# Two output projections computed third by third, with the feed-forward norm cut into parts between the products

## What is computed

```python
for li in range(2):
    h = rmsnorm(y, attn_norm[li])
    m = mixer_ab(h, ...) if li == 0 else mixer_c(h, ...)   # both end with  out @ w_out  (1024 x 1024)
    y = y + m                                              # <- the output projection
    y = y + swiglu(rmsnorm(y, ffn_norm[li]), ffn_w_in[li], ffn_w_out[li])   # <- the norm after it
y = rmsnorm(y, final_norm)

def rmsnorm(x, g):
    return x * rsqrt(mean(x * x, axis=-1) + 1e-6) * g
```

## Time and profile before

| | |
|---|---|
| three timed runs | 3367.0 us median, 3360.1 to 3375.76 us |
| profiled execution | span 3367.8 us; the page gives no time for it apart from the span |
| TensorE | 3161.1 us busy, 94% of the span |
| VectorE, ScalarE, GpSimd busy | 1456.8, 727.1, 96.9 us |
| chain that ended last | TensorE has 89% of it, VectorE 5% |

### The profile page before, as it was taken

The page is one execution under the profiler, slowest core; times in us unless marked ns, Lnnn a source line. Parts: engine busy times, 40 slices in busy tenths (PEclk is TensorE's granted clock), DMA queues, the critical chain, the costliest instruction groups (busy, mean ns, idle before and its releaser), DMA issues.

```text
span 3367.8 us, 45153 instructions
## 1 busy us (share of the span) xinstructions
PE 3161.1 (94%) x17988; PEld 3004.2 (89%) x17988; DVE 1456.8 (43%) x2451; ACT 727.1 (22%) x1160; POOL 96.9 (3%) x88
## 2 busy tenths in 40 slices
PE   6997989997999999999899999996979999999997
PEld 5996456797999999999799999996979999999996
DVE  6887333325333333333545455454352333333335
ACT  3121445513111111111311111220131111111111
POOL 3000000001000000000100000000010000000001
PEclk9998958998999999999899999996989999999998
DMA  3112410110111111110201111100201111111111
GB/s 120 45 44 70 153 41 1 69 44 32 45 41 41 44 44 44 44 39 32 94 33 39 39 40 39 40 33 21 100 26 56 38 39 45 44 39 44 38 44 57
DMA packets 47748, 163.11 MB, mean 48 GB/s; under 512 B 8416, under 2 KB 15888, under 8 KB 44768
## 3 DMA queue, kind: packets, MB, share of 16 engines
q1 hardware_dynamic: 42992, 148.45, 13.1%
q10 hardware_dynamic: 3456, 8.91, 0.7%
q0 software_dynamic: 1136, 3.27, 0.5%
HBM read 143.28 MB, written 18.92 MB: 48 GB/s over the span
## 4 chain that ended last, share of the span: by engine, by line
PE 89%; DVE 5%; issue 2%; ACT 2%; POOL 1%; DMA 1%; DVEq 0%; POOLq 0%; ACTq 0%; SPq 0%
PE PS L513 19%; PE PS L514 19%; PE PS L515 19%; PE PS L755 5%; PE PS L757 5%; PE PS L756 5%; PE PS L1406 4%; PE PS L1136 2%; PE PS L1167 2%; DVE HF L624 1%; PE PS L1149 1%; PE PS L1160 1%; PE PS L1118 1%; POOL SQ L425 1%; DVE HBL L634 1%
## 5 line engine op out<-in xcount | busy, mean ns | idle before, releaser
L513 PE MATMUL PS<-HAH,WH 128*128 128x384 f32 x1872 | 649.6, 347 | 27.0 <-issue 9.7
L514 PE MATMUL PS<-HAL,WH 128*128 128x384 f32 x1872 | 634.4, 339 | 0.0
L515 PE MATMUL PS<-HAH,WL 128*128 128x384 f32 x1872 | 633.8, 339 | 0.0
L513 PE MATMUL PS<-HBH,WH 128*128 128x384 f32 x1872 | 626.3, 335 | 0.0
L514 PE MATMUL PS<-HBL,WH 128*128 128x384 f32 x1872 | 626.2, 335 | 0.0
L515 PE MATMUL PS<-HBH,WL 128*128 128x384 f32 x1872 | 626.1, 334 | 0.0
L501 DVE TENSOR_TENSOR WL<-WR,WH 128x1024 fp32r<-128x1024 f32 x200 | 243.0, 1223 | 568.5 <-ACT WH L496 567.0
L513 PEld LDWEIGHTS PS<-HAH,WH 128*128 128x128 f32 x1872 | 358.4, 191 | 29.1 <-issue 19.9
L514 PEld LDWEIGHTS PS<-HAL,WH 128*128 128x128 f32 x1872 | 358.6, 192 | 9.7 <-issue 8.7
L755 PE MATMUL PS<-UH,WH 128*128 128x384 f32 x1056 | 360.3, 341 | 5.2 <-issue 5.0
L756 PE MATMUL PS<-UL,WH 128*128 128x384 f32 x1056 | 359.0, 340 | 0.0
(11 more groups left out here) (200 smaller groups left out, 2776.0 us busy)
## 6 DMA issues: line engine op xcount, KB each, us to landing
WR<-w_fi_in SPq DMA_DIRECT2D x88, 512.0 KB, 3.6
WR<-w_fo_in SPq DMA_DIRECT2D x44, 512.0 KB, 3.5
WR<-w_c_in SPq DMA_DIRECT2D x32, 512.0 KB, 4.2
WR<-w_ab_in SPq DMA_DIRECT2D x20, 512.0 KB, 3.6
CACHES<-k_cache_in SPq DMA_DIRECT2D x8, 1024.0 KB, 6.8
CACHES<-v_cache_in SPq DMA_DIRECT2D x8, 1024.0 KB, 5.0
X<-x_t_in SPq DMA_DIRECT2D x3, 1536.0 KB, 10.7
x_spill<-X SPq DMA_DIRECT2D x1, 4608.0 KB, 12.3
```

The costliest lines, as they stand in the source:

```text
L513: nc.tensor.matmul(out, wh, hh(k, third(n)), start=(k == 0), stop=False)
L514: nc.tensor.matmul(out, wh, hl(k, third(n)), start=False, stop=False)
L515: mm = nc.tensor.matmul(out, wl, hh(k, third(n)), start=False, stop=(k == KT - 1))
```

## The change

The projection now goes third by third. For third 0 all 8 output blocks run, then for third 1, then for third 2: 24 products in straight code, with no loop. The weights of every block are therefore loaded, and cut into high and low parts, three times (24 loads of 512 KB instead of 8 in each layer), and each load serves one product. Two PSUM banks take turns (3 and 4) instead of six.

While third n is projected, the norm of third n-1 runs in parts, one part behind each product: m=0 folds the last squares and sums, m=1 takes the root, makes the diagonal and spreads it, m=2 and m=3 scale, m=4 and m=5 split high and low; m=4 to m=7 square and fold what is finished of the running third. VectorE does all folds; GpSimd's `fold_pair` is now called twice instead of four times. The norm of third 2 falls into the first block of the feed-forward part, whose products stand in a new order: a0, sums, b0, spread, a1, b1, a2, b2.

```diff
         def proj_sp(sp, T, w):
-            with sp.Fori(0, KT // 2 - 1) as i:
...
+            for p in range(2, N3 * KT):
+                weights(sp, T, p % 2, w[p % KT, :, :])
...
-            for norm in range(4):
-                fold_pair(2 * N3 + N3 + norm * 2 * N3)
+            for norm in range(2):
+                fold_pair(2 * N3 + N3 + 3 * N3 + norm * (2 + 3) * N3)
...
         def proj_pe(pe, T, ready):
...
+            for p in range(N3 * KT):
+                n, m = divmod(p, KT)
+                have(pe, T, p % 2)
+                if m == 0:
+                    ready(n)
+                need(pe, s_x, T("x") - 1)
+                T.add("x")
+                product(PS[:, 3 + p % 2, 0:TH], p % 2, n).then_inc(s_xo, 1)
+                if n and m == 0:
+                    rms_sums(pe, T, n - 1)
+                if n and m == 1:
+                    rms_cast(pe, T, n - 1)
+
+        SQ_PARTS = (slice(0, 4), slice(4, 6), slice(6, 8))
+
+        def part_squares(act, T, n, part):
+
+            act.wait_ge(s_x, T("x0") + n * KT + SQ_PARTS[part].stop)
+            if part == 0:
+                need(act, s_ms, T("ms"))
+                T.add("ms")
+            ks = SQ_PARTS[part]
+            act.activation(SQ[:, ks, :], X[:, ks, third(n)], ACT.Square).then_inc(s_sq, 1)
+
+        def part_root(act, T, n):
+            act.wait_ge(s_ms, T("ms"))
...
+        def part_hi(act, T, n, half):
+            hf = HF1 if n % 2 else HF0
+            out = (HAH, HBH)[half]
+            T.add("hf")
+            act.wait_ge(s_hf, T("hf"))
+            act.activation(out[:, :, third(n)], hf[:, half * AB:(half + 1) * AB, :], ACT.Copy).then_inc(s_hhi, 1)
+
+        def proj_act(act, T, stored=None):
+
+            T.add("x0", T("x") - T("x0"))
+            for p in range(N3 * KT):
+                n, m = divmod(p, KT)
+                cut_hi(act, T, 1 - p % 2, None if p == 0 else (s_xo, T("x")))
+                T.add("x", 1)
+                if p == 4 and stored:
+                    stored()
+                if n and m == 0:
+                    part_squares(act, T, n - 1, 2)
+                if n and m == 1:
+                    part_root(act, T, n - 1)
+                if n and m == 3:
+                    part_hi(act, T, n - 1, 0)
+                if n and m == 4:
+                    part_hi(act, T, n - 1, 1)
+                if m == 4:
+                    part_squares(act, T, n, 0)
+                if m == 6:
+                    part_squares(act, T, n, 1)
+
+        def part_fold(dve, T, part):
...
+        def proj_dve(dve, T, reloaded, gain):
+            for p in range(N3 * KT):
+                n, m = divmod(p, KT)
+                cut_lo(dve, T, 1 - p % 2)
+                if n and m == 0:
+                    part_fold(dve, T, 2)
+                if n and m == 1:
+                    rms_diag(dve, T, n - 1)
+                if n and m == 2:
+                    rms_scale(dve, T, n - 1, gain, False, range(0, AB))
+                if n and m == 3:
+                    rms_scale(dve, T, n - 1, gain, False, range(AB, KT))
+                if n and m == 4:
+                    rms_lo(dve, T, n - 1, (0,))
+                if n and m == 5:
+                    rms_lo(dve, T, n - 1, (1,))
+                if m == 6:
+                    part_fold(dve, T, 0)
+                if m == 7:
+                    part_fold(dve, T, 1)
+                if p in (0, 2):
+                    dve.wait_ge(s_xr[p // 2], 16 * reloaded)
+                T.add("x")
+                need(dve, s_xo, T("x"))
+                xs = X[:, m, third(n)]
+                dve.tensor_tensor(xs, xs, PS[:, 3 + p % 2, 0:TH], ALU.add).then_inc(s_x, 1)
...
-        def ffn_pe(pe, T, ready):
+        def ffn_pe(pe, T, base):
+            def first_block():
+                have(pe, T, 0)
+                for n in range(N3):
+                    pe.wait_ge(s_hlo, base + 2 * (n + 1))
+                    need(pe, s_si, T("fj") - 2)
+                    T.add("fj")
+                    product(PS[:, n, 0:TH], 0, n).then_inc(s_fa, 1)
+                    if n == 0:
+                        rms_sums(pe, T, 2)
+                        have(pe, T, 1)
+                        need(pe, s_x, T("x"))
+                    need(pe, s_u, T("fb") - 2)
+                    T.add("fb")
+                    product(PS[:, 3 + n, 0:TH], 1, n).then_inc(s_fb, 1)
+                    if n == 0:
+                        rms_cast(pe, T, 2)
...
-        def ffn_act(act, T):
+        def ffn_act(act, T, base):
+            def last_norm():
+                part_squares(act, T, 2, 2)
+                cut_hi(act, T, 2, (s_xo, T("x")))
+                part_root(act, T, 2)
+                part_hi(act, T, 2, 0)
+                part_hi(act, T, 2, 1)
+                act.wait_ge(s_hlo, base)
...
-        def ffn_dve(dve, T, gain, final):
+        def ffn_dve(dve, T, last, gain, final):
+            def last_norm():
+                part_fold(dve, T, 2)
+                cut_lo(dve, T, 2)
+                rms_diag(dve, T, 2)
+                dve.wait_ge(s_hlo, T("hlo") - 2)
+                rms_scale(dve, T, 2, last, False)
+                rms_lo(dve, T, 2)
```

More of the change, by code:

```diff
@@ L616, in rms_diag, with rms_scale @@
                               ALU.mult).then_inc(s_dg, 1)
-        def rms_scale(dve, T, n, gain, final):
-            T.add("rb")
-            dve.wait_ge(s_rb, T("rb"))
+        def rms_scale(dve, T, n, gain, final, ks=range(KT)):
+            if 0 in ks:
+                T.add("rb")
+                dve.wait_ge(s_rb, T("rb"))
             hf = HF1 if n % 2 else HF0
-            for k in range(KT):
+            for k in ks:
                 out = X[:, k, third(n)] if final else hf[:, k, :]
@@ L627, in rms_scale, with rms_lo @@
                     ins.then_inc(s_hf, 1)
-        def rms_lo(dve, T, n):
+        def rms_lo(dve, T, n, halves=(0, 1)):
             hf = HF1 if n % 2 else HF0
             for half, hi, lo in ((0, HAH, HAL), (1, HBH, HBL)):
+                if half not in halves:
+                    continue
                 T.add("hhi")
@@ new lines, in encoder @@
+        SQ_PARTS = (slice(0, 4), slice(4, 6), slice(6, 8))
[8 more added lines that the diff above has]
+            act.wait_ge(s_ms, T("ms"))
+            act.activation(rt[:, 3 * n:3 * n + 3], PS[:, n, TH:TH + TPT], ACT.Sqrt,
+                           bias=eps[:, 0:1], scale=1.0 / D).then_inc(s_rt, 1)
@@ new lines, in part_fold @@
+        def part_fold(dve, T, part):
+            T.add("sq")
+            dve.wait_ge(s_sq, T("sq"))
+            if part == 0:
+                link(dve, T, dve.tensor_tensor(SQ[:, 0:2, :], SQ[:, 0:2, :], SQ[:, 2:4, :], ALU.add))
+                link(dve, T, dve.tensor_tensor(SQ[:, 0, :], SQ[:, 0, :], SQ[:, 1, :], ALU.add))
+            else:
+                link(dve, T, dve.tensor_tensor(SQ[:, 2 * part + 2, :], SQ[:, 2 * part + 2, :], SQ[:, 2 * part + 3, :], ALU.add))
+                ins = dve.tensor_tensor(SQ[:, 0, :], SQ[:, 0, :], SQ[:, 2 * part + 2, :], ALU.add)
+                if part == 1:
+                    link(dve, T, ins)
+                else:
+                    ins.then_inc(s_ps, 1)
@@ L734, in w_in @@
                 for j in range(2):
+                    if first and j == 0:
+                        first_block()
+                        continue
                     have(pe, T, sa[j])
                     for n in range(N3):
-                        if first and j == 0:
-                            ready(n)
                         need(pe, s_si, T("fj") - 2)
@@ L797, in w_in @@
                         cut_hi(act, T, 1, (s_xo, T("x")))
+                        if first:
+                            last_norm()
                     elif first:
@@ L808, in w_in @@
                     if j == 0:
-                        cut_hi(act, T, 2, (s_xo, T("x")))
+                        if not first:
+                            cut_hi(act, T, 2, (s_xo, T("x")))
                     elif first:
@@ L838, in w_in @@
                     cut_lo(dve, T, 1 if j == 0 or first else 0)
-                    if j == 0:
+                    if j == 0 and first:
+                        last_norm()
+                    elif j == 0:
                         cut_lo(dve, T, 2)
@@ L1781, in _ @@
             proj_pe(pe, T, both)
-            norm_pe(pe, T)
-            ffn_pe(pe, T, normed(pe, T, H_ABO))
+            ffn_pe(pe, T, H_ABO)
             norm_pe(pe, T, begun=True)
@@ L1786, in _ @@
             proj_pe(pe, T, lambda n: pe.wait_ge(s_hlo, H_C + 2 * (n + 1)))
-            norm_pe(pe, T)
-            ffn_pe(pe, T, normed(pe, T, H_CO))
+            ffn_pe(pe, T, H_CO)
             norm_pe(pe, T, begun=True, final=True)
@@ L1803, in _ @@
             proj_act(act, T)
-            norm_act(act, T, lambda n: X_AB - N3 + n + 1)
-            act.wait_ge(s_hlo, H_F0)
-            ffn_act(act, T)
+            ffn_act(act, T, H_F0)
```

(15 more changed lines are left out.)

## The result

| | median of four runs | lowest to highest | profiled execution: span, TensorE busy, VectorE busy |
|---|---|---|---|
| before | 3365.08 us | 3360.1 to 3375.76 | 3367.8, 3161.1, 1456.8 us |
| after | 3316.92 us | 3313.82 to 3318.18 | 3316.4, 3143.6, 1501.0 us |

The ratio is 0.9854 (95%: 0.9836 to 0.9873): faster by 48 us, where 35 were forecast. That the number falls on that rival's is luck.

The account below looks back on a forecast made before the run. TensorE, with 89% of the chain that ended last, was taken to bound the kernel. Terms -32.0 - 31.5 + 9.5 + 1.8 + 16.7 = -35.5 us gave a forecast of 3332 us, 8-in-10 range 3316 to 3350.

Parts of the forecast that it names:

- that rival's: Start of the projections: third weights come early, the queue serving them beside the large X load; 3316 us, chance 0.08.
- holes behind the projections: TensorE's idle and slow-clock time in norm and first six feed-forward products: 32.0 us saved in layer 0, 31.5 in layer 1.
- sums and spread, six times: Norm work left on TensorE between products: 1.58 us for each third, 9.5 us added over both layers.
- layer 0, third weights: Layer 0's projection start: TensorE waits 1.8 us for the third weights, queued behind 4.6 MB of X.
- layer 1, second cut: Layer 1's second projection product waits 1.7 us for its weights, whose VectorE cut stands behind six low parts.
- layer 1, third weights: Layer 1's third projection product waits 13.1 us for weights that land 15.0 us after issue.
- layer 1, restart: Layer 1's projection: after the long idling for the third weights, TensorE's restart is charged at 1.9 us.
- third 2 not covered: Norm of third 2 in the first feed-forward block: taken as hidden by 0.4 us, 0 cost; rival up to 3362 us.
- the feed-forward loop's jumps in E: From layer 1's seventh feed-forward product to the kernel's end: no change from the loop's jumps, 0 us.
- behind that loop's end: Matmuls just behind the end of layer 1's feed-forward loop: no change counted, 0 us.
- The rival of the clock lost at each product: Projection: TensorE loses its clock at each wait, 91 us over 48 products, 3423 us; chance of slower 0.07.
- The loops are gone ... I count 0 in both directions: Projections: unrolling their loops neither gains nor costs time, 0 us, as the looped projection already showed TensorE fully busy.

Follow-up runs that it names:

- run 8: The changed kernel run and profiled once more, nothing altered: 3319.5 us, ratio 0.9862.
- run 5: The changed kernel with the first feed-forward block in the old order (a0, a1, a2, b0, b1, b2): 3337.94 us, ratio 0.992.
- run 1: The kernel before, run and profiled once more, unchanged: 3374.81 us.
- run 2: The kernel before with the loops of both projections written out, order of work unchanged: 3360.43 us, ratio 0.9981.
- run 3: The kernel before with eight idle matmuls on TensorE in the norm of layer 1: 3357.59 us, ratio 0.9976.
- run 7: The kernel before with 64 idle one-column matmuls on TensorE in the norm of layer 1: 3383.85 us, ratio 1.006.
- run 6: The kernel before with only the projection third by third and weights loaded three times, norm left behind it: 3379.84 us, ratio 1.0036.
- run 4: The changed kernel with third weights loaded ahead of the reloads of X, and blocks 2 to 7 reloaded by thirds: 3308.28 us, ratio 0.9823.

## Why the prediction was right and where it was wrong

| term | forecast | measured | how |
|---|---|---|---|
| holes behind the projections | -32.0, -31.5 | gone | the six products take 26.28 in each layer: 24.96 and a third's sums and spread |
| sums and spread, six times | +9.5 | +7.9 | 1.32 each |
| layer 0, third weights | +1.8 | +1.7 | 667.53 - 661.71 - 4.16 |
| layer 1, second cut | +1.7 | +1.7 | 7.76 - 6.05 of the earlier trace rows |
| layer 1, third weights | +13.1 | +11.7 | 15.86 - 4.16 |
| layer 1, restart | +1.9 | +2.5 | 2361.88 - 2355.22 - 4.16; 2.0 in run 8, 1.9 in run 5 |
| third 2 not covered | 0 | 0 | run 5: about 10 a layer if it were not |
| the feed-forward loop's jumps in E | 0 | -7.4 | runs 1, 2, 3, 7 |
| behind that loop's end | 0 | -1.3 | open |

**Right.** What bounds the kernel, where the hole goes and what takes its place. The engines' parts fit, and neither VectorE nor the weights were late in steady state: in each layer TensorE waits for weights at the second or third product and nowhere else. The rival of the clock lost at each product fell with this. Early weights fell too: the landing was 13.8 us in both layers.

**Mis-sized.** The third weights of layer 1 (the landing behind the reload took 13.8 and not the 15.0 of the earlier trace rows, 1.2 of the 1.4 missing) and the sums and spreads: they were priced from rows that hold a wait, and a matmul starts before the last ends: the sums cost 697.37 - 692.62 - 4.16 = 0.59, not 0.83. The cover of third 2, when taken away, costs 9.5 to 10.1 a layer rather than the 7.6: the wait ahead of a2 is 7.8, and behind it the matmuls start 0.32 us apart until 781.10, which adds 2.1. The prediction itself has two prices for this, 15 us for both layers in the part on the norm and 15 in each layer among the rivals; run 5 gives 20 for both.

**Wrong: the step "The loops are gone ... I count 0 in both directions".** For the loops that went it holds (run 2: B and D unchanged). It fails since the step looked at the removed loops alone: E was put at 0 and came out at -8.8, 7.4 of them at the jumps of a loop that stayed. A loop that stays has a price that depends on where it lies in the code, and unrolling 18 products ahead of it moves it. The trace of before showed the 8.6 us of "issue" in eight waits; the prediction does not use that row, since it lay outside of the two places. It would have given a bound of about 10 us to gain. Forecast and span differ by 15.9 us: E 8.8, D and B 2.4, A and C 4.7.

**Open.** The 1.3 us behind the loop's end in layer 1: the matmuls 0.32 us apart stand there in before and runs 1, 2, 3, 6 and 7, and in none of after and runs 4, 5 and 8, so moved code alone did not remove them. At the same place in layer 0 they come and go between two executions of one kernel: the clock of the 3 us behind the wait is 1.00 in before (1599.9 to 1602.9) and 0.71 in run 1 (1599.2 to 1602.2). Whether the change did it in layer 1 is not shown. A and C: their difference of 2.8 and 1.9 lies within their scatter between executions (6.9 and 12.0 us), so none of it is put down to the change; what makes them scatter was not tried. C holds the same feed-forward loop of layer 0, and there the change moved it the other way: TensorE's waits for "issue" at its jumps are 1.0 us in two before and 1.9 in four after. The profiled execution's time stands 1.7 us above its span (3318.18 against 3316.4), which the forecast took as 0.

## What to carry to other kernels

A norm that stands between two products can be cut into parts of one product's length, as long as each engine's part fits beside what it already does for the product; the last part needs products of its own to hide behind. Look in the DMA queue for what a small, urgent load stands behind: putting it ahead of 4.6 MB of bulk, with the bulk cut into thirds, was worth another 11.5 us in one layer here. When a change makes the code longer or shorter ahead of a hardware loop, look at the waits for "issue" at the loop's jumps before and after: they can move by 2 us a jump with no work changed, and an experiment that adds or removes code has to watch for that.

## What the runs showed of the hardware that was not expected

The jump of a hardware loop cost TensorE up to 1.4 us over a steady matmul (0.5 to 0.7 in the kernel after), and another 1.6 to 2.1 us six matmuls on, if the loop lay badly; eight idle matmuls ahead of it took the second wait away and with 64 it was there again. The trace has the fetches behind this, as packets of 16 KB on an instruction queue, about one in 20 us of steady matmuls and more at a jump. The three-round loops of the projections showed no such price. What a wait costs the product behind it, 4.16 us when steady, differs from execution to execution: after 11.4 to 11.6 us of waiting it took 6.06 to 6.65 us (after, runs 5, 6 and 8), after 5.8 us 6.05 to 6.73 (before, runs 1, 2, 3 and 7), after 1.5 us 4.29 (after, layer 0) and after 1.76 us 5.85 (run 6, layer 0). The granted clock shows it: 0.57 from 2355.2 to 2361.2 in after, and 1.00 from 2361.2 on.
